# A trunk kernel of two layers: the experts' ring of split weight granules has eight slots instead of six, the ring of raw granules eight instead of twelve

## What is computed

```python
def swiglu(t, w_gate, w_up, w_down):
    return (jax.nn.silu(t @ w_gate) * (t @ w_up)) @ w_down

def moe_swiglu(x, w_router, w_gate, w_up, w_down):
    ...
    logits = (t @ w_router).astype(jnp.float32)
    top_vals, top_idx = lax.top_k(logits, TOP_K)
    top_w = jax.nn.softmax(top_vals, axis=-1)
    ...
    for e in range(N_EXPERTS):
        out = out + gates[:, e:e + 1].astype(t.dtype) * swiglu(t, w_gate[e], w_up[e], w_down[e])
```

## Time and profile before

| | |
|---|---|
| median of 3 runs | 1212.9 us (1212.29 to 1213.69) |
| the profiled execution: its own time, its span | 1211.82 us, 1210.1 us |
| mean granted clock of TensorE | 0.988 of full speed |
| busy: PE, DVE, ACT | 1158.7, 879.2, 755.0 us |
| read from HBM | 292.9 MB |

### The profile page before, as it was taken

How to read it: one execution, slowest core, us unless ns; L and a number is a source line. 1 busy time by engine, 2 the same in 40 slices (tenths; PEclk the granted TensorE clock), 3 DMA queues, 4 the chain that set the end, 5 groups by cost and what they waited for, 6 DMA issues and landing times.

```text
span 1210.1 us, 15835 instructions
## 1 busy us (share of the span) xinstructions
PE 1158.7 (96%) x5641; PEld 968.4 (80%) x5641; DVE 879.2 (73%) x989; ACT 755.0 (62%) x905; POOL 19.4 (2%) x60
## 2 busy tenths in 40 slices
PE   7999999999999999999999999999999999999994
PEld 6887788888888878887788889878887888788863
DVE  5468667665455455586666778998998899889994
ACT  6546556555444435555666447887778787877881
POOL 2000000000000001000000000000000000000000
PEclk9999999999999999999999989999999999999997
DMA  9655522668555445647225639999999999999990
GB/s 317 221 165 174 165 72 103 197 215 294 180 196 178 146 136 172 193 115 227 94 77 176 226 109 331 375 394 387 363 377 357 395 365 373 360 391 370 365 361 38
DMA packets 120010, 294.97 MB, mean 244 GB/s; under 512 B 8974, under 2 KB 33644, under 8 KB 119420
## 3 DMA queue, kind: packets, MB, share of 16 engines
q1 hardware_dynamic: 118832, 288.66, 67.6%
q0 software_dynamic: 960, 5.28, 1.2%
q10 hardware_dynamic: 140, 0.04, 0.0%
HBM read 292.90 MB, written 1.05 MB: 243 GB/s over the span
## 4 chain that ended last, share of the span: by engine, by line
PE 76%; DVE 10%; ACT 7%; issue 5%; DMA 1%; SPq 0%; DVEq 0%; ACTq 0%; POOLq 0%; POOL 0%
PE bank L1457 21%; PE bank L1459 20%; PE bank L1458 20%; DVE w_lo L1253 5%; PE bank L1833 3%; ACT w_hi L798 3%; PE bank L1834 3%; PE bank L1495 1%; DMA raw<-in_w_in 1%; ACT w_hi L620 1%; PE bank L1816 1%; PE bank L1656 1%; PE bank L1636 1%; PE bank L1779 1%; ACT p_buf L743 1%
## 5 line engine op out<-in xcount | busy, mean ns | idle before, releaser
L1253 DVE TENSOR_TENSOR w_lo<-raw,w_hi 128x1792 fp32r<-128x1792 f32 (+3 forms) x198 | 383.4, 1963 | 48.3 <-ACT w_hi L798 47.0
L798 ACT ACTIVATE w_hi<-raw 128x1792 fp32r<-128x1792 f32 (+3 forms) x198 | 325.7, 1659 | 100.0 <-PE bank L1459 73.5
L967 DVE TENSOR_TENSOR w_lo<-raw,w_hi 128x1536 fp32r<-128x1536 f32 (+3 forms) x144 | 242.8, 1692 | 180.3 <-ACT w_hi L620 179.8
L620 ACT ACTIVATE w_hi<-raw 128x1536 fp32r<-128x1536 f32 (+4 forms) x144 | 205.5, 1433 | 160.6 <-PE bank L1459 157.8
L1457 PE MATMUL bank<-w_hi,aT_hi 128*128 128x512 f32 (+1 forms) x592 | 235.8, 398 | 5.5 <-DVE aT_lo L998 3.4
L1459 PE MATMUL bank<-w_hi,aT_lo 128*128 128x512 f32 (+1 forms) x592 | 230.7, 390 | 0.0
L1458 PE MATMUL bank<-w_lo,aT_hi 128*128 128x512 f32 (+1 forms) x592 | 230.3, 389 | 0.0
L1457 PEld LDWEIGHTS bank<-w_hi,aT_hi 128*128 128x128 f32 x592 | 111.7, 189 | 27.9 <-DVE w_lo L967 3.1
L1459 PEld LDWEIGHTS bank<-w_hi,aT_lo 128*128 128x128 f32 x592 | 111.4, 188 | 22.8
L1458 PEld LDWEIGHTS bank<-w_lo,aT_hi 128*128 128x128 f32 x592 | 111.8, 189 | 20.5
L1833 PE MATMUL bank<-w_hi,xT 128*128 128x448 f32 x256 | 96.4, 377 | 4.8 <-DVE w_lo L1253 4.5
(11 more groups left out here) (271 smaller groups left out, 1548.6 us busy)
## 6 DMA issues: line engine op xcount, KB each, us to landing
raw<-in_moe_w_gate SPq DMA_DIRECT2D x128, 448.0 KB, 6.0
raw<-in_moe_w_up SPq DMA_DIRECT2D x128, 448.0 KB, 5.5
raw<-in_moe_w_down SPq DMA_DIRECT2D x112, 512.0 KB, 6.3
raw<-in_w_in SPq DMA_DIRECT2D x40, 768.0 KB, 4.5
raw<-in_dense_w_gate SPq DMA_DIRECT2D x22, 512.0 KB, 4.0
raw<-in_dense_w_up SPq DMA_DIRECT2D x22, 512.0 KB, 4.8
raw<-in_dense_w_down SPq DMA_DIRECT2D x11, 1024.0 KB, 4.9
raw<-in_w_in SPq DMA_DIRECT2D x20, 512.0 KB, 4.8
```

The lines of the kernel that those rows point to most:

```text
L620: act.activation(w_hi[:, weight_slot(b, j), 0:n], raw[:, b % 2, j, 0:n], ACT.Copy).then_inc(hi_made[j], 1)
L798: act.activation(split_of(hi_slot, m), raw_of(i, n), ACT.Copy).then_inc(e_hi_made, 1)
L967: dve.tensor_tensor(w_lo[:, s, 0:n], raw[:, b % 2, j, 0:n], w_hi[:, s, 0:n].bitcast(F32), ALU.subtract).then_inc(lo_made[j], 1)
L1253: dve.tensor_tensor(split_of(lo_slot, m), raw_of(i, n), split_of(hi_slot, m).bitcast(F32), ALU.subtract).then_inc(e_lo_made, 1)
```

## The change

The two rings trade room: raw keeps eight of its twelve slots (6 to 11, 0 and 1, by RAW_AT), and the other four (16 KB per partition) become two slots of w_hi and two of w_lo (w_hi_more, w_lo_more). So the DMA of granule i now waits for the split of granule i - 8, and ACT's split of a pair for PE's use of the pair four before it. A fourth pair (granules 6 and 7) is split ahead: by ACT behind the exponential of the router (L849), by DVE behind `gate_weights`.

```diff
-RAW_SLOTS, W_SLOTS, SLOT_W = 12, 6, 1024
+RAW_SLOTS, W_SLOTS, SLOT_W = 8, 8, 1024
+RAW_AT = (6, 7, 8, 9, 10, 11, 0, 1)
...
-        raw = place("raw", [P, 2, 3, SLOT])
+        raw, _, w_hi_more, w_lo_more = regions(
+            [("raw", [P, 2, 3, SLOT])],
+            [("raw_pad", [P, 2, SLOT_W]), ("w_hi_more", [P, 2, SLOT_W], F32R), ("w_lo_more", [P, 2, SLOT_W], F32R)])
...
-        hi_slot, lo_slot = (b[:, :, :].rearrange("p j (u n) -> p (j u) n", n=SLOT_W) for b in (w_hi, w_lo))
+        hi_slot, lo_slot = (
+            [(b[:, :, :].rearrange("p j (u n) -> p (j u) n", n=SLOT_W), n) for n in (2, 3, 4, 5, 0, 1)] + [(more, 0), (more, 1)]
+            for b, more in ((w_hi, w_hi_more), (w_lo, w_lo_more)))
...
-            at_slot = (i + RAW_SLOTS // 2) % RAW_SLOTS
+            at_slot = RAW_AT[i % RAW_SLOTS]
...
             i, n = SPLITS[m]
-            at_slot = (i + 2) % W_SLOTS
-            return slots[:, at_slot:at_slot + n, 0:granule_width(GRANULES[i][2])]
+            of, at_slot = slots[i % W_SLOTS]
+            return of[:, at_slot:at_slot + n, 0:granule_width(GRANULES[i][2])]
...
                             if RAW_BEFORE[i] is None:
-                                s = (i + RAW_SLOTS // 2) % RAW_SLOTS
-                                sp.wait_ge(lo_made[s % 6 // 2], MIX[1] + (BLK_MIX, BLK_MIX + 1)[s < RAW_SLOTS // 2] + 1)
+                                s = RAW_AT[i]
+                                sp.wait_ge(lo_made[s % 6 // 2], MIX[1] + (BLK_MIX, BLK_MIX + 1)[s < 6] + 1)
...
                     if W_BEFORE[i] is None:
-                        act.wait_ge(used[i // 2], MIX[1] + BLK_MIX + 2)
+                        if i < 6:
+                            act.wait_ge(used[i // 2], MIX[1] + BLK_MIX + 2)
+                        else:
+                            act.wait_ge(lo_made[1], MIX[1] + BLK_MIX + 2)
...
                 act.activation(rt[:, t, 5, 0:1], rt[:, t, 4, 0:1], ACT.Exp, scale=rstd[3][:, t:t + 1]).then_inc(lexp_made, 1)
+            expert_hi(6)
...
                     expert_lo(4)
                     gate_weights()
+                    expert_lo(6)
                     count_overflow()
```

More of the change, by code:

```diff
@@ L402, in w_of @@
         def w_of(slots, i):
-            return slots[:, (i + 2) % W_SLOTS, 0:granule_width(GRANULES[i][2])]
+            of, at_slot = slots[i % W_SLOTS]
+            return of[:, at_slot, 0:granule_width(GRANULES[i][2])]
         def wait_x_read(eng, r, what):
```

## The result

The change made the kernel slower: 1241.4 us in the median of four runs (1238.6 to 1243.6), the kernel before beside it 1212.6 us (1212.0 to 1213.7). The ratio is 1.0236, 95% interval 1.0218 to 1.0253. Forecast were 1202 us and a range up to 1221; what came is the rival of the raw ring, at more than its price. In the code after, ACT's split is L808, DVE's L1264, the fold L890, the DMA issue L542.

The account below looks back on a forecast made before the run. PE, DVE and perhaps loads were taken as nearly full, the split ring as too short. 11.7 + 1.0 + 2.0 + 0.8 - 1.2 - 0.7 - 2.0 = 11.6 us, taken as 11: 1202 us, range 1190 to 1221.

Parts of the forecast that it names:

- What bounds the kernel: Experts: PE, DVE and perhaps loads nearly full; split ring too short between uneven partners; PE stands 29.1 us, no load waits.
- Two more split slots: PE finds each w_lo one split earlier: 11.7 us in three repeats, 1.0 and 2.0 at the edges, 0.8 at the start.
- Four raw slots fewer: Experts' loads are issued later: costs 1.2 us over the repeats, 0.7 to 791 us, 2.0 in the last stretch.
- The 410 GB/s: Rate of the fullest stretches (785 to 795 us), against 374 GB/s asked: the same bytes do fit.
- The Trainium skill: Estimate of 4.1 us for two granules' loads; by it eight raw slots cost nothing, sum 3.9 us lower, near 1198.
- The slower rival: Raw ring of eight becomes the bound: 2.65 against 2.59 us a pair, +11 us, 1224 us; chance 0.20.
- The signs: Experts: w_lo waits under 12 us, fold +0.5 to 1, landing some 5; wrong if ACT waits over 15 for loads.
- No change: Fold, hidden values and late loads take back the gain except 2.7 us three times; loads take 8: 1212 us; chance 0.16.
- all waits go: Earlier PE brings ACT's and DVE's gates forward too; up to 29.1 us go, 1186 us or so; chance 0.14.

Follow-up runs that it names:

- e7: Kernel before with ten raw slots instead of twelve, six split slots kept: 1213.9 us, ratio 1.0008.
- e2: Changed kernel with ten raw slots instead of eight, eight split slots kept: 1200.7 us, ratio 0.9893 to the kernel before.
- e1: Kernel before with the raw ring cut from twelve to eight slots, six split slots kept: 1242.6 us, ratio 1.0238.
- e13: Kernel before (twelve raw, six split slots) with every split cut into two of one granule: 1192.7 us, ratio 0.9837.
- e15: Kernel before with eight raw slots instead of twelve, six split slots, and every split cut into two of one granule: 1192.5 us, ratio 0.9836.

## Why the prediction was wrong

- **What bounds the kernel.** Right for before, but that the full stretch is 15 of the page's slices, not 18. The reading that "the raw ring covers" the loads was right at twelve slots and at ten (e7).
- **Two more split slots**, 11.7 + 1.0 + 2.0 + 0.8 = 15.5 us. The mechanism is right where loads are in time: 13.2 us from e7 to e2, and PE's waits for w_lo fall from 30.0 us, those without a name counted, to 3.2 in e2. In the changed kernel they are 9.0 us in the lines that name w_lo, under 12 as said, but 19.8 with the others (the prediction's 29.1 us had counted these). With the raw ring of eight the two slots are worth nothing (e1 against after), which the sum could not see, since it added terms that don't add.
- **Four raw slots fewer**, 3.9 us. This is the step that failed. Alone it cost 2.4% or 29 us (e1 against before), all of it between ten and eight slots (28.7, e1 against e7), and 40.7 with the split ring's gain that it takes along (e2 against after). Three parts of it were wrong. First, "the landing follows the number in flight", and with eight slots there would be fewer: the number fell from 4.67 to 4.21 only, and the mean landing from 6.01 to 5.74 us, not to 5. Loads alone, four slots issued in pairs, need 5.4 us already at 288 GB/s, so 5 wasn't to be had at 374. The 4.1 us at 966 to 976 us is the landing with 3.1 in flight, where the kernel drew 330 GB/s and loads alone, three in flight, 314; it goes with a rate that the experts can't live on. Second, 6.4 us for a pair's load left out the 0.32 us between ACT and DVE and the 0.36 until SP has issued again. Third, "mean balance" was held against three short places only; a ring whose circuit is longer than four times what its consumers take for a pair loses on every pair: 10.90 us for 10.3.
- **The 410 GB/s** of the fullest stretches as a sign that "the same bytes do fit": loads alone reach 406 with five in flight. The bandwidth was there, the slots to ask for it weren't.
- **The Trainium skill** (SBUF — State Buffer, The DMA setup-cost knee), an estimate of 4.1 us for two granules: with just two in flight the loads alone agree, 4.1 us in the median. At the four to five in flight that the experts' rate takes they need 4.8 to 5.6, in the kernel 5.7; for that the estimate is too low, and the measurement decides.
- **The slower rival** was right in mechanism, in its sign (the median stayed above 5.5 us) and in its circuit: 10.6 us forecast, 10.90 measured. It was priced low, +11 for +28.8, because it set 2.65 us against 2.59. It is 2.73 against 2.58.
- **The signs.** ACT waits for loads by 60 us or more where 15 were to prove me wrong. The median landing from 802 to 921 us stayed at 5.8 us. The fold's wait rose by 17 us, not by 0.5 to 1.
- **No change, and all waits go:** neither came. Even e2 gained less than the 26 us of the latter; e13 and e15 came close to it by another way.

What stays open: why one larger DMA for a pair makes the kernel slower, why more split slots are worse where loads are in time (ten than eight in place, eight than six with single splits), how the loss divides between the ring alone and the work beside it, and the last 1.4 us of the 28.8.

## What to carry to other kernels

A ring's pace is its circuit (issue, landing, every hold until the slot is free) divided by its slots; work it out against what the consumers need before slots are taken away, and take the landing at the rate that you need, not the shortest in the trace. Here 10.9 us without slack, at the 2.49 us to a pair that the ten slots of e2 reach, want 4.4 pairs: five pairs cost nothing, four cost 29 us. Where memory is short, release by smaller pieces first: splits of one granule cost DVE 7% more for each, and gave 20 us with twelve raw slots and 50 with eight. And where a wait shows (PE for the fold) isn't where it is made: reordering that line of work gave nothing.

## What the runs showed of the hardware

- Loads of 448 KB alone: 223, 314, 380, 406 GB/s with 2, 3, 4 and 5 in flight, and 407 with 6 and 8; landings of 4.1, 4.4, 4.8, 5.6, 6.8 and 9.0 us. The DMA share is 0.78 already at 223 GB/s.
- Issued in pairs, up to four in flight give 288 GB/s, up to six 406.
- One DMA of 896 KB for two of 448 KB: 345 for 355 and 365 GB/s in the ring alone with eight slots, 406 with ten either way; in the kernel a pair is in after 6.64 us for 6.61, and the kernel takes 12.5 us more.
